# The up projection's entrance in another order: two snapshots at once, the norm's sums behind the fourth product, its spread behind the seventh

## Chip, core and metric

The kernel runs on one core of a Trainium2 chip. What counts is the device time of one execution in microseconds (us), the median over the runs shown; lower is better.

## What is computed

The reference is a whole block of a network on 1024 tokens of width 1024: a mixer with a residual, a gated feed-forward part with a short convolution, then a second block with latent attention and a Fourier mixer. The change lies where the feed-forward part begins:

```python
def rmsnorm(x, g, eps=EPS):
    xf = x.astype(jnp.float32)
    y = xf * lax.rsqrt(jnp.mean(xf * xf, axis=-1, keepdims=True) + eps)
    return (y * g.astype(jnp.float32)).astype(x.dtype)

def conv_ffn(h, w_up, conv_w, conv_b, w_down):
    gu = h @ w_up
    gate, up = gu[..., :D_FF], gu[..., D_FF:]
    gate = lax.conv_general_dilated(
        gate, conv_w[:, None, :], window_strides=(1,), padding=[(CONV_WIDTH - 1, 0)],
        dimension_numbers=('NWC', 'WIO', 'NWC'), feature_group_count=D_FF) + conv_b
    return (jax.nn.gelu(gate, approximate=False) * up) @ w_down

# in first_block
        x = x + merged @ w_out[l]
        x = x + conv_ffn(rmsnorm(x, ffn_norm_g[l]), w_up[l], conv_w[l], conv_b[l], w_down[l])
```

## The kernel before

Everything lies feature-major: 128 features on the partitions, 1024 tokens along the row. A float32 matrix product is made of three passes of matmuls over a high and a low part (`PASSES`), the high part being a rounded copy of the operand and the low part what is left of it. ScalarE (ACT) makes the high parts, VectorE (DVE) the low parts of the activations, GpSimd (POOL) the low parts of the weights (L689).

The up projection works in 22 pairs `p` of two 128-column blocks, one of the gate and one of the up half. Each pair is a 2 by 2 block product that is done with seven products of sums instead of eight. So a pair is seven products of 12 matmuls of 128x512 each (L1032), numbered n = 0 to 6 in the code; in words they are called product 1 to product 7 here. Product n multiplies `WS[n]` (weight sums, high and low part) with `OPERANDS[n]` (B11, BT1, B21, B22, BT2, BT4, BT3; BT are sums of quarters Y of the activations). Pairs take turns between two sets of three PSUM banks. Products 1, 5 and 7 add up in one bank, 2 and 4 in a second, 3 and 6 follow each other in the third. That is why copies and additions stand between them:

- ACT's `snap` copies a bank after product 1 (to FIRST), 2 (to KEEP), 5 and 6. Product 4 waits for the second snapshot, since it goes on adding in the bank of product 2 (`st_snap`, in `up_pair` of the tensor block).
- DVE's first addition of a pair (L2614, `GATE` from the bank of product 3 and FIRST) frees that bank. Product 6 opens it anew, so it waits for this addition: `pe.wait_ge(st_free, p * 3 + 7)`. The second addition (L2619) completes the other half of GATE, and L2622 multiplies it with the norm's factor, which PE has spread over all partitions in PSUM (`pair(3)`). From there go on the convolution (ACT L1812, DVE L2624 and L2626) and the gelu (L1817).

The norm's factor does not stand in the way of the products: they run on x times the gain, and the result is scaled afterwards. For it the squares are summed up in ACC; PE sums over the partitions with 8 narrow matmuls (`norm_sum`, L766), DVE turns the sum to a mean (L2592), ACT takes the root, DVE takes the reciprocal (L2597) and writes it on two diagonals (L2119), and PE spreads these (`norm_spread`, L774). GATE occupies the room in SBUF in which ACC lay, KEEP of the first pair that of Y22, and FIRST that of x.

Each engine runs its own list in the order in which the code writes it. The entrance is the stretch between the last matmuls of the output projection (L733) and the second pair's first product. On the tensor queue stand in a row: products 1 and 2, the norm sums, products 3 and 4, the spread, products 5 to 7, then the second pair. On DVE stand: the last sums of activations (L2508), low parts of BT2, mean, low parts of BT4, reciprocal, two diagonals, low parts of BT3, a memset, two sums of weights of the second pair (L2491, L2494), then the first addition. `late_hi` and `late_lo` are the high and low parts of BT2, BT4 and BT3, `high_part` those of `WS`, and `weight_sums` the sums from which WS are cast.

Of the kernel before, what the change touches and what calls it, by code (L numbers as in the profile page):

```python
# [10 lines left out]
ACT = mybir.ActivationFunctionType  # L11
# [3 lines left out]
T = 1024  # L15
D = 1024
KC = D // P
# [10 lines left out]
HK = KC // 2  # L28
FG = 8
HALF = T // 2  # L30
# [60 lines left out]
def before(phase, what):  # L91

    total = 0
    for name, adds in PHASES:
        if name == phase:
            return total
        total += adds.get(what, 0)
    raise KeyError(phase)
# [104 lines left out]
def build(nc, t_in, out):  # L203
# [105 lines left out]
    GATE = SC[:, 2:2 + T]  # L309
# [68 lines left out]
    lo = sem("lo")  # L378
# [74 lines left out]
    def operand_at(n, k):  # L453

        if n < 2:
            return 2 * k + n
        if n < 4:
            return 2 * HK + 2 * k + n - 2
        return 4 * HK + 2 * (n - 4) + k // 2
# [254 lines left out]
    def _(pe):  # L714
# [299 lines left out]
        def up_pair(p, q, first=False):  # L1014

            pe.wait_ge(st_free, p * 3 + 3)
            for n in range(PRODUCTS):
                if first and n == 2:
                    take(1, b("up", 1))
                pe.wait_ge(w_st, p * PRODUCTS + (n + 1))  # L1020
                if n == 3:
                    pe.wait_ge(st_snap, p * 4 + 2)
                elif n == 5:
                    pe.wait_ge(st_free, p * 3 + 7)
                elif n == 6:
                    pe.wait_ge(st_snap, p * 4 + 3)
                bank = BANKS[q][n]
                for k in range(HK):
                    if first:
                        pe.wait_ge(lo, before("out1", "split") + operand_at(n, k) + 1)  # L1030
                    for wp, xp in PASSES:
                        mm = pe.matmul(PS[:, bank:bank + HALF], WS[n][:, (wp * HK + k) * P:(wp * HK + k + 1) * P],  # L1032
                                       OPERANDS[n][:, (xp * HK + k) * HALF:(xp * HK + k + 1) * HALF],
                                       start=OPENS[n] and k == 0 and wp == 0 and xp == 0, stop=k == HK - 1 and wp == 1,
                                       skip_group_check=True)
                mm.then_inc(st_prod, 1)
                if first and n == 1:
                    norm_sum(before("norm2", "norm"), before("norm2", 2), early=before("norm2", "square") - 1)
                elif first and n == 3:
                    norm_spread(before("norm2", "norm"), before("norm2", 3))  # L1040

        take(0, b("up", 0))
# [425 lines left out]
    def _(act):  # L1468
# [232 lines left out]
        def attn_residual():  # L1701

            def operand_hi(dst, k, src):
                act.activation(dst[:, k * HALF:(k + 1) * HALF], src, ACT.Copy, scale=v1("ffn_g", k + (HK if dst is B21 or dst is B22 else 0))
                               ).then_inc(hi, 1)

            for c in range(KC):
                k, x, g = c % HK, TMP[c % 2], v1("ffn_g", c)
                pieces = ((B11, Y11), (None, Y12)) if c < HK else ((B21, Y21), (B22, Y22))
                for half in range(2):  # L1710
                    part = slice(half * HALF, (half + 1) * HALF)
                    dst, y = pieces[half]
                    if half == 0 or c == KC - 1:
                        act.wait_ge(x_new, before("out1", "xnew") + c + half + 1)
                    if dst is not None:
                        operand_hi(dst, k, x[:, part])
                    act.activation(y[:, k * HALF:(k + 1) * HALF], x[:, part], ACT.Copy, scale=g).then_inc(y_done, 1)
                    if c == KC - 1:
                        act.activation(SQ[:, part], x[:, part], ACT.Square).then_inc(sq_ready, 1)
                if c < KC - 1:  # L1720
                    act.activation(SQ, x, ACT.Square).then_inc(sq_ready, 1)
                if c == KC - 2:
                    high_part(0, 0, 0)
                    high_part(0, 1, 0)
                if c < HK:
                    act.wait_ge(t_sum, c + 1)
                    act.activation(BT1[:, k * HALF:(k + 1) * HALF], Y11[:, k * HALF:(k + 1) * HALF], ACT.Copy
                                   ).then_inc(hi, 1)
# [18 lines left out]
        def late_hi(n, sums):  # L1747

            dst, src = ((BT2, Y22), (BT4, Y21), (BT3, Y12))[n]
            for j in range(2):  # L1750
                part = slice(j * T, (j + 1) * T)
                act.wait_ge(t_sum, sums[j])
                act.activation(dst[:, part], src[:, part], ACT.Copy).then_inc(hi, 1)
# [22 lines left out]
        def snap(p, n, dst, bank):  # L1776
            act.wait_ge(st_prod, p * PRODUCTS + n)
            act.activation(dst, PS[:, bank:bank + HALF], ACT.Copy).then_inc(st_snap, 1)

        def ff_high(p, q, kept=None):  # L1780

            act.wait_ge(xt, p + xts[0] + 1)
            if kept is not None:
                act.wait_ge(st_prod, PRODUCTS * (FFC - 1) + 1)
            dst = FFS[q] if kept is None else FFD[kept]
            act.activation(dst[:, 0:T], PROD, ACT.Copy).then_inc(hi, 1)

        def up_pair(p, q, spilled=True, last=False, kept=None):

            def high_parts(first, end):  # L1790
                if not last:
                    for n in range(first, end):
                        high_part(p + 1, n, 1 - q)

            b_at, c_at, a_at = SUM_AT[q]
            snap(p, 1, FIRST[q], b_at)
            high_parts(0, 1)
            if isinstance(p, int) and p == 0:
                act.wait_ge(lo, before("out1", "split") + operand_at(4, HK - 1) + 1)
            if spilled:  # L1800
                act.wait_ge(ff_out, p * 16 - 16)
            snap(p, 2, KEEP[q][:, HALF:T], c_at)
            if isinstance(p, int) and p == 0:
                phase_norm("norm2")
                late_hi(2, (T3_SUMS[1], T3_SUMS[3]))
            else:
                ff_high(p - 1, 1 - q, kept)
            high_parts(1, 3)
            snap(p, 5, GATE[:, HALF:T], b_at)
            high_parts(3, 5)  # L1810
            act.wait_ge(gn_ready, p + 1)
            act.activation(CONV, SC[:, 0:T], ACT.Copy, scale=vec[:, bass.ds(p + VEC["conv0"], 1)]).then_inc(tap_ready, 1)  # L1812
            snap(p, 6, KEEP[q][:, 0:HALF], a_at)
            high_parts(5, 7)
            act.wait_ge(cv_ready, p + 1)
            act.wait_ge(lo, p + before("up", "split"))
            act.activation(PROD, CONV, ACT.Gelu, bias=vec[:, bass.ds(p + VEC["conv_b"], 1)]).then_inc(gl_ready, 1)  # L1817

        high_part(0, 2, 0)
        high_part(0, 3, 0)  # L1820
        late_hi(0, (T2_SUMS[1], T2_SUMS[3]))
        high_part(0, 4, 0)
        late_hi(1, (T4_SUMS[1], T4_SUMS[3]))
        high_part(0, 5, 0)
        high_part(0, 6, 0)
        act.wait_ge(done[2], before("norm2", 2) + 1)
        act.wait_ge(x_out, 16 * KC)
        up_pair(0, 0, spilled=False)
        act.wait_ge(lo, before("up", "split"))
        up_pair(1, 1, spilled=False)  # L1830
# [232 lines left out]
    def _(v):  # L2063
# [453 lines left out]
        def attn_residual():  # L2517
# [14 lines left out]
            def add_square(part):  # L2532
                sqs[0] += 1
                acs[0] += 1
                v.wait_ge(sq_ready, sqs[0])
                v.tensor_tensor(ACC[:, part], ACC[:, part], SQ[:, part], ALU.add).then_inc(sq_added, 1)
                v.wait_ge(sq_added, acs[0])
# [32 lines left out]
            v.wait_ge(y_done, 2 * c + 1)  # L2570
            operand_lo(B21, Y21, k * HALF, HALF)
            new_x(c, 1)
            add_square(halves[0])
            v.wait_ge(done[1], before("up", 1))
            weight_sums(0, 0, (2, 4))
            v.wait_ge(y_done, 2 * c + 2)
            operand_lo(B22, Y22, k * HALF, HALF)
            add_square(halves[1])
# [6 lines left out]
        def late_lo(dst, src):  # L2585
            for j in range(2):
                operand_lo(dst, src, j * T, T)

        v.wait_ge(t_sum, ts[0])
        late_lo(BT2, Y22)  # L2590
        v.wait_ge(done[2], before("norm2", 2) + 1)
        v.tensor_scalar(stat[:, 0:QT_N], PS[:, 2048:2048 + QT_N], 1.0 / D, 1e-6, ALU.mult, ALU.add).then_inc(ms_ready, 1)  # L2592
        v.wait_ge(ms_ready, before("norm2", "norm") + 1)
        v.sem_inc(free[2], 1)
        late_lo(BT4, Y21)
        v.wait_ge(sd_ready, before("norm2", "norm") + 1)
        chain(v.reciprocal(stat[:, 0:QT_N], stat[:, 0:QT_N]))  # L2597
        for a in (0, 4):
            diagonal(DIAG[:, a * P:(a + 4) * P], stat, a, a + 4).then_inc(diag_ready, 1)
        late_lo(BT3, Y12)  # L2600

        chain(v.memset(SC[:, 0:2], 0.0))

# [40 lines left out]
            v.tensor_tensor(dst[:, T:2 * T], PROD, dst[:, 0:T].bitcast(F32), ALU.subtract).then_inc(lo, 1)  # L2644
            v.wait_ge(lo, p + his[0] + 1)

        weight_sums(1, 1, (1, 3))
        up_pair(0, 0)
        up_pair(1, 1)
        with v.Fori(1, FFC // 2 - 1) as i:  # L2650
# [564 lines left out]
```

## Time and profile before

| | us |
|---|---|
| median of 3 runs | 2555.14 (2554.55 to 2556.97) |
| the profiled execution, its own time | 2560.54 |
| its span | 2558.7 |
| PE busy in it | 2468.8 (96%) |
| DVE busy | 1513.8 (59%) |
| ACT busy | 868.5 (34%) |
| POOL busy | 758.0 (30%) |

Times in the rows are us from the start of the span. The profiled execution took 5.4 us longer than the median; stretches are compared inside the trace and their difference is then laid on the median. In the timeline a row begins with its start and its length; matmuls overlap, so a row of twelve is 0.16 us longer than the step to the next product. The granted clock is a share of full speed, 1.00 for 2.4 GHz and 0.50 for 1.2 GHz.

### The profile page before, as it was taken

Reading aid. Unit: us, or ns where it says so; the run is one execution under the profiler, and the core shown is the slowest. Engines: PE = TensorE matmul, PEld = TensorE weight load, DVE = VectorE, ACT = ScalarE, POOL = GpSimd, SP = SyncE. Lnnn points to the kernel's source line nnn. Section 1 sums busy time; section 2 is a strip of 40 time slices with the busy share of each in tenths; the row PEclk is TensorE's granted clock in tenths of the full one; section 3 lists DMA queues with packets and bytes.
Section 4 is the critical chain, followed back from the end, with each engine's and each line's share of the span. In section 5 each row is a group of like instructions: output and inputs, shape, how many; then the busy total and the mean of one; then the engine's idle time right before and its main releaser. Section 6 shows DMA issues by size and latency. Waiting matters only on the chain.

```text
span 2558.7 us, 33196 instructions
## 1 busy us (share of the span) xinstructions
PE 2468.8 (96%) x12060; PEld 2035.9 (80%) x12060; DVE 1513.8 (59%) x1981; ACT 868.5 (34%) x1290; POOL 758.0 (30%) x442
## 2 busy tenths in 40 slices
PE   7999999999999999999999979999999989899997
PEld 5777787787787888888888868788888878688886
DVE  7856674735557877777411663377777764633454
ACT  4232222223224544445100232156666651222121
POOL 3232232332333555555344412200000003222221
PEclk9999999999999999999999989999999999999999
DMA  5134243421422223233553211100000002111112
GB/s 181 42 115 140 99 149 108 140 74 50 164 107 107 99 107 123 98 113 133 222 194 135 77 41 33 58 1 17 8 8 8 9 9 62 32 40 33 41 41 74
DMA packets 54417, 210.70 MB, mean 82 GB/s; under 512 B 6420, under 2 KB 7700, under 8 KB 49082
## 3 DMA queue, kind: packets, MB, share of 16 engines
q1 hardware_dynamic: 50340, 194.92, 22.0%
q10 hardware_dynamic: 3990, 14.59, 1.6%
q8 instruction: 57, 0.93, 0.1%
q14 instruction: 30, 0.25, 0.0%
HBM read 173.30 MB, written 38.55 MB: 83 GB/s over the span
## 4 chain that ended last, share of the span: by engine, by line
PE 84%; DVE 9%; issue 4%; ACT 1%; DMA 1%; POOL 1%; DVEq 0%; SPq 0%; ACTq 0%; POOLq 0%
PE PS L733 39%; PE PS L1032 16%; PE PS L1061 9%; PE PS L1277 4%; PE PS L1210 3%; PE PS L1216 2%; PE PS L1249 2%; PE PS L891 1%; PE PS L926 1%; DVE cols L2777 1%; PE PS L1200 1%; DVE SC L2327 1%; PE PS L766 1%; PE PS L774 1%; PE PS L1427 1%
## 5 line engine op out<-in xcount | busy, mean ns | idle before, releaser
L733 PE MATMUL PS<-H,w_hl 128*128 128x512 f32 x4512 | 1070.1, 396 | 31.8 <-DVE H L2142 9.4
L733 PEld LDWEIGHTS PS<-H,w_hl 128*128 128x128 f32 x4512 | 847.6, 190 | 231.7 <-issue 33.5
L682 POOL CAST w_hl<-w_raw 128x1024 fp32r<-128x1024 f32 x138 | 155.1, 1124 | 1546.7 <-PE PS L733 1011.8
L684 POOL TENSOR_TENSOR w_hl<-w_raw,w_hl 128x1024 fp32r<-128x1024 f32 x138 | 348.2, 2523 | 11.0
L1032 PE MATMUL PS<-BT,WS 128*128 128x512 f32 x1056 | 247.0, 389 | 0.0
L1061 PE MATMUL PS<-FFD,w_hl 128*128 128x512 f32 x1056 | 239.8, 389 | 0.1
L1032 PEld LDWEIGHTS PS<-BT,WS 128*128 128x128 f32 x1056 | 198.2, 188 | 41.6 <-issue 0.5
L1061 PEld LDWEIGHTS PS<-FFD,w_hl 128*128 128x128 f32 x1056 | 198.1, 188 | 41.6 <-DVEq L2450 0.5
L1032 PE MATMUL PS<-B,WS 128*128 128x512 f32 x792 | 190.7, 395 | 3.6 <-issue 3.6
L1032 PEld LDWEIGHTS PS<-B,WS 128*128 128x128 f32 x792 | 151.1, 191 | 35.7 <-issue 4.0
L689 POOL TENSOR_TENSOR WS<-w_raw,WS 128x512 fp32r<-128x512 f32 x88 | 140.3, 1605 | 73.1 <-ACT WS L1745 72.8
L1210 PE MATMUL PS<-CKV,QN 128*128 128x512 f32 (+1 forms) x576 | 142.1, 364 | 0.2 <-DVE PT L2793 0.2
L689 POOL TENSOR_TENSOR WS<-SUM,WS 128x512 fp32r<-128x512 f32 x66 | 98.3, 1503 | 122.3 <-ACT WS L1745 122.3
L2444 DVE TENSOR_TENSOR X<-PS,X 128x1024 f32 (+2 forms) x33 | 39.4, 1192 | 143.2 <-PE PS L1061 142.5
L1277 PE MATMUL PS<-PT,CKT 128*128 128x256 f32 x960 | 120.7, 283 | 1.5 <-DVE PT L2793 1.5
L1277 PEld LDWEIGHTS PS<-PT,CKT 128*128 128x128 f32 x960 | 117.8, 191 | 2.4 <-DVE PT L2793 1.7
L2793 DVE TENSOR_TENSOR PT<-PS,PT 128x512 fp32r<-128x512 f32 (+1 forms) x192 | 103.6, 596 | 23.5 <-ACT PT L1932 22.6
L1932 ACT ACTIVATE PT<-PS 128x512 fp32r<-128x512 f32 (+1 forms) x192 | 86.7, 523 | 76.1 <-PE PS L1249 76.1
L1210 PEld LDWEIGHTS PS<-CKV,QN 128*128 128x128 f32 x576 | 98.6, 188 | 17.3 <-DVE PT L2793 1.2
L2777 DVE TENSOR_REDUCE cols<-PS 128x1 f32<-128x1280 f32 x64 | 95.4, 1491 | 26.2 <-PE PS L1216 25.6
L1919 ACT ACTIVATE E<-PS,cols 128x1280 f32<-128x1280 f32 x64 | 85.3, 1333 | 51.6 <-DVE cols L2778 51.6
L1216 PE MATMUL PS<-KPE,QPS 128*128 128x512 f32 (+1 forms) x384 | 100.1, 355 | 0.0
(341 smaller groups left out, 3005.2 us busy)
## 6 DMA issues: line engine op xcount, KB each, us to landing
w_raw<-in_units SPq DMA_DIRECT2D x186, 512.0 KB, 3.6
AW<-in_ada SPq DMA_DIRECT2D x48, 512.0 KB, 4.2
ff_part<-FFS SPq DMA_DIRECT2D x20, 1024.0 KB, 4.9
FFD<-ff_part SPq DMA_DIRECT2D x20, 1024.0 KB, 5.6
X<-in_x SPq DMA_DIRECT2D x8, 512.0 KB, 8.7
x_part<-SC SPq DMA_DIRECT2D x8, 512.0 KB, 2.6
X<-x_part SPq DMA_DIRECT2D x4, 1024.0 KB, 8.7
out<-X SPq DMA_DIRECT2D x16, 256.0 KB, 2.1
```

The lines of the kernel that those rows point to most:

```text
L682: pool.tensor_copy(hi_part, raw).then_inc(w_hi, 1)
L684: pool.tensor_tensor(lo_part, raw, hi_part.bitcast(F32), ALU.subtract).then_inc(w_split, 1)
L689: pool.tensor_tensor(lo_part, ADDENDS[q][n][:, :], hi_part.bitcast(F32), ALU.subtract).then_inc(w_st, 1)
L733: mm = pe.matmul(PS[:, out_at + a:out_at + a + m], w(s, wp, w0 + k), src[:, o:o + m], start=(k == 0 and wp == 0 and xp == 0), stop=(k == k ...
L1032: mm = pe.matmul(PS[:, bank:bank + HALF], WS[n][:, (wp * HK + k) * P:(wp * HK + k + 1) * P], OPERANDS[n][:, (xp * HK + k) * HALF:(xp * HK ...
L1061: mm = pe.matmul(PS[:, out_at + a:out_at + a + 512], w(s, wp, w0 + k), FFD[home][:, xp * T + a:xp * T + a + 512], start=(k == 0 and wp == ...
L1210: mm = pe.matmul(PS[:, base + a:base + a + m], QN[:, qp_ * T + t * P:qp_ * T + (t + 1) * P], CKV[:, kp_ * TK + a:kp_ * TK + a + m], start= ...
L1216: mm = pe.matmul(PS[:, base + a:base + a + m], QPS[:, t * P:(t + 1) * P], KPE[:, kp_ * TK + a:kp_ * TK + a + m], start=False, stop=(kp_ == 1))
L1277: mm = pe.matmul(PS[:, 3584:3584 + GQ], CKT[:, vp * TK + kb * P:vp * TK + (kb + 1) * P], PT[:, xp * PTW + kb * GQ:xp * PTW + (kb + 1) * GQ ...
L1932: act.activation(block_cols(0, t, k0, k1), bank_cols(bank, k0, k1), ACT.Copy).then_inc(pt_hi, 1)
L2777: chain(v.tensor_reduce(cols[:, 22 + t % 2:23 + t % 2], PS[:, base:base + TK], AX, ALU.max))
L2793: v.tensor_tensor(block_cols(1, t, k0, k1), bank_cols(bank, k0, k1), block_cols(0, t, k0, k1).bitcast(F32), ALU.subtract).then_inc(pt_lo, 1)
```

## The change

It moves instructions on three engines and adds one copy on ACT; on PE and DVE nothing is added or removed. The norm sums go behind product 4 (n == 3, the fourth counted from one), the spread behind product 7 (n == 6). ACT casts WS[2] before the last half of x arrives, takes the snapshots of products 1 and 2 one behind the other as soon as the last x has been read, the second one into the spare FIRST[1], and copies it to KEEP later; the root comes behind the snapshot of product 5. DVE makes two sums of weights ahead of an addition of squares, all six low parts of BT2, BT4 and BT3 in a row ahead of the mean, and the second pair's sums of weights between mean and reciprocal. The first addition stays last.

```diff
@@ up_pair of the tensor block
-                if first and n == 1:
+                if first and n == 3:
                     norm_sum(before("norm2", "norm"), before("norm2", 2), early=before("norm2", "square") - 1)
-                elif first and n == 3:
+                elif first and n == 6:
                     norm_spread(before("norm2", "norm"), before("norm2", 3))
@@ scalar block, attn_residual
                         act.activation(SQ[:, part], x[:, part], ACT.Square).then_inc(sq_ready, 1)
+                        high_part(0, 2 + half, 0)
@@ scalar block, up_pair
-            snap(p, 1, FIRST[q], b_at)
-            high_parts(0, 1)
             if isinstance(p, int) and p == 0:
-                act.wait_ge(lo, before("out1", "split") + operand_at(4, HK - 1) + 1)
-            if spilled:
-                act.wait_ge(ff_out, p * 16 - 16)
-            snap(p, 2, KEEP[q][:, HALF:T], c_at)
-            if isinstance(p, int) and p == 0:
+                snap(p, 5, GATE[:, HALF:T], b_at)
                 phase_norm("norm2")
-                late_hi(2, (T3_SUMS[1], T3_SUMS[3]))
+                high_parts(0, 5)
             else:
...
@@ scalar block, ahead of the first pair
-        high_part(0, 2, 0)
-        high_part(0, 3, 0)
+        act.wait_ge(x_out, 16 * KC)
+        act.wait_ge(sq_ready, before("norm2", "square"))
+        snap(0, 1, FIRST[0], SUM_AT[0][0])
+        snap(0, 2, FIRST[1], SUM_AT[0][1])
         late_hi(0, (T2_SUMS[1], T2_SUMS[3]))
         high_part(0, 4, 0)
         late_hi(1, (T4_SUMS[1], T4_SUMS[3]))
         high_part(0, 5, 0)
         high_part(0, 6, 0)
+        late_hi(2, (T3_SUMS[1], T3_SUMS[3]))
+        act.wait_ge(lo, before("out1", "split") + operand_at(4, HK - 1) + 1)
+        chain(act.activation(KEEP[0][:, HALF:T], FIRST[1], ACT.Copy))
         act.wait_ge(done[2], before("norm2", 2) + 1)
-        act.wait_ge(x_out, 16 * KC)
         up_pair(0, 0, spilled=False)
@@ vector block
             new_x(c, 1)
-            add_square(halves[0])
             v.wait_ge(done[1], before("up", 1))
             weight_sums(0, 0, (2, 4))
+            add_square(halves[0])
...
         late_lo(BT2, Y22)
+        late_lo(BT4, Y21)
+        late_lo(BT3, Y12)
         v.wait_ge(done[2], before("norm2", 2) + 1)
...
-        late_lo(BT4, Y21)
+        weight_sums(1, 1, (1, 3))
         v.wait_ge(sd_ready, before("norm2", "norm") + 1)
...
-        late_lo(BT3, Y12)
...
-        weight_sums(1, 1, (1, 3))
         up_pair(0, 0)
```

The tensor queue at the entrance, one piece of the difference (B_103 to BT_109 are the seven operands, WS_114 to WS_120 the seven weights of the first pair):

```order
 L1032 MATMUL PS<-B_103,WS_114 128x512 x12
 L1032 MATMUL PS<-BT_104,WS_115 128x512 x12
-L766 MATMUL PS<-ones,SC 128x1 x8
 L1032 MATMUL PS<-B_105,WS_116 128x512 x12
 L1032 MATMUL PS<-B_106,WS_117 128x512 x12
-L774 MATMUL PS<-SC,ones 128x512 x2
+L766 MATMUL PS<-ones,SC 128x1 x8
 L1032 MATMUL PS<-BT_107,WS_118 128x512 x12
 L1032 MATMUL PS<-BT_108,WS_119 128x512 x12
 L1032 MATMUL PS<-BT_109,WS_120 128x512 x12
+L774 MATMUL PS<-SC,ones 128x512 x2
 L1032 MATMUL PS<-B_103,WS_114 128x512 x12
```

The sums now stand behind product 4, the spread behind product 7, right ahead of the second pair.

DVE before, from the low parts of BT2 to the first addition (Y_110, Y_112 and Y_113 are Y12, Y22 and Y21; stat holds the mean; w_raw_124 and SUM_121 belong to the second pair; SC holds GATE and FIRST):

```order
L2514 TENSOR_TENSOR BT_107<-Y_112,BT_107 128x1024 x2
L2592 TENSOR_SCALAR stat<-PS 128x8
L2514 TENSOR_TENSOR BT_108<-Y_113,BT_108 128x1024 x2
L2597 RECIPROCAL stat<-stat 128x8
L2119 TENSOR_TENSOR SC<-ident,stat 128x512 x2
L2514 TENSOR_TENSOR BT_109<-Y_110,BT_109 128x1024 x2
```

The same place in the changed kernel:

```order
L2518 TENSOR_TENSOR BT_107<-Y_112,BT_107 128x1024 x2
L2518 TENSOR_TENSOR BT_108<-Y_113,BT_108 128x1024 x2
L2518 TENSOR_TENSOR BT_109<-Y_110,BT_109 128x1024 x2
L2598 TENSOR_SCALAR stat<-PS 128x8
L2495 TENSOR_TENSOR SUM_121<-w_raw_124 128x512
L2498 TENSOR_TENSOR w_raw_124<-w_raw_124 128x512
```

The low parts moved ahead of the mean, and two sums of weights stand between the mean and the reciprocal; behind them follow reciprocal, diagonals, memset and the first addition.

## Rows read from the trace of the kernel before

**Rows 1.** The page, busy time of each engine over the span.

```profile
PE 2468.8 (96%) x12060; PEld 2035.9 (80%) x12060; DVE 1513.8 (59%) x1981; ACT 868.5 (34%) x1290; POOL 758.0 (30%) x442
```

**Rows 2.** The chain that ended last, 770 to 860 us: start, length, what.

```profile
825.54 34.50 PE PS L1032 x152
```

**Rows 3.** PE's timeline, 770 to 850 us: start, length, instructions, idle before.

```profile
802.22 2.88 PE L1032 MATMUL PS<-B,WS 128*128 128x512 f32 x12
...
807.66 0.94 PE L766 MATMUL PS<-ones,SC 128*128 128x1 f32 x8
809.31 1.35 PE L766 MATMUL PS<-ones,SC 128*128 128x1 f32 x8 [0.70 <-DVEq L2579]
810.52 4.32 PE L1032 MATMUL PS<-B,WS 128*128 128x512 f32 x12
818.47 5.35 PE L1032 MATMUL PS<-B,WS 128*128 128x512 f32 x12 [3.63 <-issue]
823.66 1.88 PE L774 MATMUL PS<-SC,ones 128*128 128x512 f32 x4
...
833.58 2.88 PE L1032 MATMUL PS<-B,WS 128*128 128x512 f32 x12
```

**Rows 4.** Windows of 1 us: length, PE busy, granted clock, DMA share, GB/s.

```profile
809.00:810.00 1.00, 0.69 (x6) 0.95 0.00 0
...
813.00:814.00 1.00, 1.00 (x5) 0.84 0.57 123
...
816.00:817.00 1.00, 0.00 (x0) 0.87 0.43 172
...
823.00:824.00 1.00, 1.00 (x4) 0.72 0.44 176
```

**Rows 5.** ACT's timeline: a square of x, snapshots of products 2, 5 and the next 2.

```profile
802.13 0.61 ACT L1719 ACTIVATE SC<-SC 128x512 f32<-128x512 f32 x1
...
817.79 0.58 ACT L1778 ACTIVATE KEEP<-PS 128x512 f32<-128x512 f32 x1
...
828.34 0.60 ACT L1778 ACTIVATE SC<-PS 128x512 f32<-128x512 f32 x1 [1.22 <-PE PS L1032]
...
839.22 0.60 ACT L1778 ACTIVATE KEEP<-PS 128x512 f32<-128x512 f32 x1
```

**Rows 6.** The last spill of x on the SP queue, and its time to landing.

```profile
804.64 0.33 SPq L558 DMA_DIRECT2D x_part<-SC  x1
...
x_part<-SC SPq DMA_DIRECT2D x1, 512.0 KB, 2.6
```

**Rows 7.** DVE's timeline, 803 to 845 us.

```profile
803.33 0.68 DVE L2514 TENSOR_TENSOR B<-Y,B 128x512 fp32r<-128x512 f32 x1
...
812.35 3.46 DVE L2514 TENSOR_TENSOR BT<-Y,BT 128x1024 fp32r<-128x1024 f32 x2
815.73 0.15 DVE L2592 TENSOR_SCALAR stat<-PS 128x8 f32<-128x8 f32 x1
...
820.40 2.15 DVE L2119 TENSOR_TENSOR SC<-ident,stat 128x512 f32<-128x512 f32 x2
822.48 2.35 DVE L2514 TENSOR_TENSOR BT<-Y,BT 128x1024 fp32r<-128x1024 f32 x2
824.77 0.06 DVE L2602 MEMSET SC<- 128x2 f32 x1
825.25 0.69 DVE L2491 TENSOR_TENSOR SUM<-w_raw 128x512 f32<-128x512 f32 x1 [0.41 <-DVE SC L2602]
...
826.58 0.69 DVE L2614 TENSOR_TENSOR SC<-PS,SC 128x512 f32<-128x512 f32 x1
...
831.02 1.22 DVE L2622 TENSOR_TENSOR SC<-SC,PS 128x1024 f32<-128x1024 f32 x1
...
844.26 0.69 DVE L2614 TENSOR_TENSOR SC<-PS,SC 128x512 f32<-128x512 f32 x1 [0.18 <-DVE FFS L2644]
```

**Rows 8.** POOL's timeline, 770 to 850 us: the low part of WS[4].

```profile
813.28 1.45 POOL L689 TENSOR_TENSOR WS<-SUM,WS 128x512 fp32r<-128x512 f32 x1 [2.96 <-ACT WS L1745]
```

More of the change, by code:

```diff
@@ L1795, in up_pair @@
             b_at, c_at, a_at = SUM_AT[q]
-            snap(p, 1, FIRST[q], b_at)
-            high_parts(0, 1)
             if isinstance(p, int) and p == 0:
-                act.wait_ge(lo, before("out1", "split") + operand_at(4, HK - 1) + 1)
-            if spilled:
-                act.wait_ge(ff_out, p * 16 - 16)
-            snap(p, 2, KEEP[q][:, HALF:T], c_at)
-            if isinstance(p, int) and p == 0:
+                snap(p, 5, GATE[:, HALF:T], b_at)
                 phase_norm("norm2")
-                late_hi(2, (T3_SUMS[1], T3_SUMS[3]))
+                high_parts(0, 5)
             else:
+                snap(p, 1, FIRST[q], b_at)
+                high_parts(0, 1)
+                if spilled:
+                    act.wait_ge(ff_out, p * 16 - 16)
+                snap(p, 2, KEEP[q][:, HALF:T], c_at)
                 ff_high(p - 1, 1 - q, kept)
-            high_parts(1, 3)
-            snap(p, 5, GATE[:, HALF:T], b_at)
-            high_parts(3, 5)
+                high_parts(1, 3)
+                snap(p, 5, GATE[:, HALF:T], b_at)
+                high_parts(3, 5)
             act.wait_ge(gn_ready, p + 1)
```

## Prediction

> **What bounds the kernel now.** The page comes first: PE is busy for 96% of the span [rows 1], so only time that PE loses or gains counts. The chain that ended last shows where: from 825.54 us on it is PE alone, product behind product [rows 2]. Whatever moves the second pair's first product, at 833.58 us, moves everything behind it. PE's timeline [rows 3] shows what the entrance costs. It begins at 802.22. Seven products at a step of 2.72 (a row of 2.88 less the overlap of 0.16) are 19.0 us, yet 31.4 pass. The rest is: the norm sums, 2.86 from 807.66 to 810.52, with a wait of 0.70 in them; 1.44 and 2.47 us that the rows of products 3 and 4 are longer than 2.88; 3.63 of idle time ahead of product 4; and the spread, from 823.66 until product 5. The clock rows [rows 4] tell why products 3 and 4 are long: the granted clock falls to 0.50 at 809.95, is back at 813.7, falls at 816.9 in the idle time and is back near 823.5. The idle time itself ends with the second snapshot, 817.79 + 0.58 = 818.37 [rows 5], so its releaser is ACT.
>
> Then the question that decides: what is late next? Product 6 began at 833.58 - 2 x 2.72 = 828.14 (ACT's snapshot of product 5, released by PE, begins at 828.34 [rows 5]), and DVE's first addition, which it waits for, had ended at 826.58 + 0.69 = 827.27 [rows 7]. That is 0.87 us of slack. So two chains reach product 6 almost together: PE's with its stalls, and DVE's list. The change shortens the first by much; I have to see what it does to the second.
>
> **Products 1 to 5.** WS[2] is cast ahead of the last half of x, in time in which ACT was idle. The snapshots wait for the last x to be spilled: issued at 804.64, 2.6 to land [rows 6], so 807.3. Product 2 ends at 807.8, both copies (0.58 each) by 809 to 809.5. Product 3 runs from 807.66 to 810.4, so product 4 starts without a wait and ends at 813.1; sums 2.15 (0.94 and 1.21 from [rows 3] without the wait), product 5 from 815.3 to 818.0, where it ended at 828.14 before. On PE alone that is 10.1 us won. If the clock falls behind the sums, 1.4 to 2.5 go, if x lands a little later, another bit: all of it costs nothing, since PE then waits.
>
> **Product 6 waits for DVE.** The changed list has the same members between the low parts of BT2 and the first addition, and the addition is still last. Its length from rows: six low parts of 1.18 (half of 2.35 [rows 7]), 7.05. GpSimd takes turns with them: the pair at 812.35 took 3.46 where the pair at 822.48, with GpSimd idle, took 2.35, so one low part of weights between two of DVE's costs 1.11. WS[4], WS[5] and WS[6] are cast by ACT in this time, so three turns, 3.3. Mean and its wait 0.3 (815.73 to 816.03). Two sums of weights 1.4. ACT's root needs the mean, and by then its table has long been loaded, so it hides behind these sums, and the reciprocal behind GpSimd. But behind the root ACT casts the second pair's WS[0] and WS[1], so two more turns of GpSimd lie around the diagonals, 2.2, and the diagonals are 1.3 (2.15 less the 0.85 of a turn in them). Memset with its wait 0.45, addition 0.7. Sum 16.7. Before it was 14.9 (812.35 to 827.27), with fewer turns of GpSimd in it.
>
> It starts when the last sum of activations is done. That was 812.3. Two sums of weights now run ahead of an addition of squares, which changes no total. ACT is free for the cast of WS[2] at about 802.65 (the square at 802.13, [rows 5]) and needs 0.6 for it, so GpSimd asks for its turn at about 803.3, and DVE's low part of B21 begins at 803.33 [rows 7]: a draw. If DVE goes first the list starts at 811.7, else at 812.6. Trace of before can't decide it; I take the middle, 812.15, and keep 0.45 to both sides. So the first addition ends at 828.85 and product 6 starts at 829.0, **0.86 later** than before: the 10.1 us have turned into idle time ahead of it.
>
> **The clock after that wait.** The idle time is 11 us; one of 3.6 sufficed for a fall [rows 4]. So product 6 begins at 1.2 GHz. The two rows at that level give 1.44 and 2.47, by how long it took to come back (2.9 and 5.1 us after the products resumed). I take 1.95, **+1.95**, bounds 1.4 and 2.9 (the last for products 6 and 7 together). Before, product 6 ran at full clock.
> The Trainium skill, TensorE: Matmul & The Clock Gate, Part 1, says the ramp is under 1% of a kernel's span and that a model need not fit it. By that the term would be dropped and the sum would be 2558.5. The rows agree on the share (0.08%), but of this change it is a third.
>
> **The spread.** It costs PE 1.76: from 823.66 to the 825.42 that lie three steps ahead of 833.58. Before it stood in the chain to product 6, now behind product 7: **+1.76** behind the wait. The second pair starts at 829.0 + 5.44 + 1.95 + 1.76 = 838.15, which is 4.57 after 833.58.
>
> **What is late next.** L2622 needs the spread. Before, the spread was done at 825.5 and L2622 ran at 831.02, when DVE came to it. Now it starts 0.17 into the second pair. From it to the end of the second pair's second snapshot it was 839.82 - 831.02 = 8.8 [rows 5, 7], over convolution and gelu; 0.15 of it waited for PE. So 8.65, and 0.1 to reach PE: 8.92 into the pair. Product 4 wants to begin at 8.16. **+0.76**. Product 6 of that pair wants the first addition: 844.95 - 831.02 = 13.93, so 14.2 into the pair, against 13.6 + 0.76: just in time. A pair later DVE has caught up.
>
> **Sum.** 0.86 + 1.95 + 1.76 + 0.76 = 5.33. On the profiled span of 2558.7 that is 2564.0; on the median, 2555.14 + 5.33 = **2560.5**. 0.2% is 5.1 us, about what a measurement of this kernel can tell from no change, so the forecast lies on this line. Lower bound: DVE wins the draw (-0.45), ACT's second cast comes too late for a turn between the diagonals (-1.1), clock 1.4 (-0.55), no stall in the second pair (-0.75): +2.5, 2557.6. Upper: +0.45, clock 2.9 (+0.95), one more turn of GpSimd in the second pair's DVE chain (+1.1): +7.8, 2563.
>
> **Rivals.**
> *Not slower: the front's gain survives.* Were the first addition done when product 5 ends, 818, the products would run through: product 7 ends at 823.5, the second pair starts at 825.2, 8.4 us sooner, 2546.8. What decides is when the addition ends: it breaks even at 828.85 - 5.33 = 823.5. For it speaks that nothing else holds PE's queue; against it that 16.7 less five turns, 11.2 us of DVE's own instructions, stand in front of the addition from 812.15 on, which is 823.3 at the very best. 4%.
> *GpSimd takes no turns.* Were the two engines not to exclude each other, the list would be 11.2 and the addition end at 823.3; the sum falls by 5.5 and the stall shrinks: about 2554.6. For it: the rows of instructions that read PSUM are not longer beside GpSimd. Against it: 3.46 beside 2.35, and 1.45 where GpSimd overlaps a low part [rows 7, 8]. 5%.
> The Trainium skill, SBUF — State Buffer, Who interferes with whom, calls this port pair an exclusive lock held for the whole instruction; the rows above agree, and by it all five turns stay.
> *DVE stays behind for longer.* With the second pair's chain late, a turn or two of GpSimd more, a stall at its product 6 too, and perhaps a fall of the clock there: 3 us on top, 2563.6. For it: DVE and GpSimd together fill most of a pair's 19 us. 13%.
> *The change doesn't do what it says*, x landing so late that product 4 still waits: worth nothing, the wait ahead of product 6 swallows up to 10 us. It is inside the forecast.
>
> **Chances.** Forecast 78%, the others as given. Inside the forecast a little over half lies above 2560.25: 41% slower, 37% same. With the third rival, slower 53%; with the second, same 42%; faster 5%. Range: the forecast's bounds, widened by the 1.2 us in which runs of before differ, and up to the third rival: 2556.4 to 2564.2.
>
> **What would show it.** Products 3 and 4 without idle time between, product 4 ending near 813; sums at 813; one idle stretch of 10 to 11 us ahead of product 6, released by DVE's first addition at 828 to 829.5; product 6 at clock 0.50 for 3 to 5 us; spread ahead of the second pair; its first product near 838; some 0.8 idle before its product 4. Wrong would be: no such idle stretch, the addition ahead of 824, or a stall in a third pair.

## The result and the profile after

The changed kernel takes 2562.31 us (median of 14, 2560.59 to 2564.24) where the kernel before, beside it, takes 2555.39 (14, 2552.89 to 2557.91): 6.9 us more, a ratio of 1.0025 with a 95% interval of 1.0017 to 1.0032. The profiled execution took 2563.18 us with a span of 2561.4.

One number is used from here on: the **entrance time**, from the start of the first pair's product 1 to the start of the third pair's product 1. Before it is 852.62 - 802.22 = 50.40 us, after it is 858.00 - 801.62 = **56.38**. So 5.98 of the 6.9 us lie in these fifty; the interval of the measurement, 4.3 to 8.2 us, holds both numbers. The two profiled spans differ by only 2.7 us, since the one of before was 5.4 above its median; the part of the traces outside the entrance is not compared here.

PE's timeline of the changed kernel, 770 to 870 us (start, length, instructions, idle before), answers to [rows 3]:

```profile
801.62 2.88 PE L1032 MATMUL PS<-B,WS 128*128 128x512 f32 x12
...
807.07 5.60 PE L1032 MATMUL PS<-B,WS 128*128 128x512 f32 x24
812.51 1.84 PE L766 MATMUL PS<-ones,SC 128*128 128x1 f32 x16
814.21 3.02 PE L1032 MATMUL PS<-BT,WS 128*128 128x512 f32 x12
828.71 7.76 PE L1032 MATMUL PS<-BT,WS 128*128 128x512 f32 x24 [11.48 <-DVEq L2620]
836.31 1.88 PE L774 MATMUL PS<-SC,ones 128*128 128x512 f32 x4
...
846.99 3.01 PE L1032 MATMUL PS<-B,WS 128*128 128x512 f32 x12 [0.60 <-ACT KEEP L1779]
...
858.00 2.88 PE L1032 MATMUL PS<-B,WS 128*128 128x512 f32 x12
```

Products 3 and 4 stand in one row of 24 without idle time, at full clock, and the sums behind them: the front of the entrance is as short as it was meant to be, and product 5 ends near 817.2. Then PE waits 11.48 us. The releaser is L2620, the semaphore that DVE raises behind its first addition. DVE's timeline of the changed kernel, over the same stretch, answers to [rows 7]:

```profile
802.73 0.68 DVE L2518 TENSOR_TENSOR B<-Y,B 128x512 fp32r<-128x512 f32 x1
...
811.20 10.21 DVE L2518 TENSOR_TENSOR BT<-Y,BT 128x1024 fp32r<-128x1024 f32 x6
821.33 0.15 DVE L2598 TENSOR_SCALAR stat<-PS 128x8 f32<-128x8 f32 x1
821.96 0.69 DVE L2495 TENSOR_TENSOR SUM<-w_raw 128x512 f32<-128x512 f32 x1 [0.48 <-DMA w_raw<-in_units]
822.69 1.64 DVE L2498 TENSOR_TENSOR w_raw<-w_raw 128x512 f32<-128x512 f32 x1
824.25 0.19 DVE L2603 RECIPROCAL stat<-stat 128x8 f32<-128x8 f32 x1
824.47 3.19 DVE L2123 TENSOR_TENSOR SC<-ident,stat 128x512 f32<-128x512 f32 x2
...
827.86 0.69 DVE L2619 TENSOR_TENSOR SC<-PS,SC 128x512 f32<-128x512 f32 x1 [0.19 <-DVE SC L2607]
...
838.22 1.22 DVE L2627 TENSOR_TENSOR SC<-SC,PS 128x1024 f32<-128x1024 f32 x1 [7.04 <-PE PS L774]
```

From 811.20 to 828.55 DVE works through its list without a longer break, and the addition is the last of it. The largest gap is 0.48 us behind the mean. Its row names a transfer of weights as releaser; the same 0.48 stands in the run with held casts with DVE's own mean as releaser, so the name is not certain. The clock, in windows of 1 us of the changed kernel (length, PE busy, granted clock, DMA share, GB/s), answers to [rows 4]:

```profile
819.00:820.00 1.00, 0.00 (x0) 0.72 0.91 168
...
832.00:833.00 1.00, 1.00 (x4) 0.50 0.00 0
833.00:834.00 1.00, 1.00 (x5) 0.96 0.00 0
```

It fell at 819.4, in the wait, and was back at 833.1, 4.4 us after product 6 began.

### The profile page after: what moved, and what is told of

Same layout as the page of the kernel before. It is cut to its first block, busy times and chain, and to the rows that moved or that the text cites. A ratio compares the mean times of both kernels' runs of the same rounds, so it can differ in the third digit from the quotient of the medians.

```text
span 2561.4 us, 33196 instructions
## 1 busy us (share of the span) xinstructions
PE 2465.3 (96%) x12060; PEld 2033.4 (79%) x12060; DVE 1514.0 (59%) x1981; ACT 868.7 (34%) x1291; POOL 756.3 (30%) x442
## 4 chain that ended last, share of the span: by engine, by line
PE 84%; DVE 11%; issue 3%; ACT 2%; DMA 1%; DVEq 0%; ACTq 0%; SPq 0%
PE PS L733 39%; PE PS L1032 16%; PE PS L1061 9%; PE PS L1277 4%; PE PS L1210 3%; PE PS L1216 2%; PE PS L1249 2%; PE PS L891 1%; PE PS L926 1%; DVE cols L2781 1%; PE PS L1200 1%; DVE SC L2331 1%; PE PS L766 1%; PE PS L774 1%; PE PS L1427 1%
## 5 line engine op out<-in xcount | busy, mean ns | idle before, releaser
L1210 PEld LDWEIGHTS PS<-CKV,QN 128*128 128x128 f32 x576 | 98.6, 188 | 16.7 <-DVE PT L2797 0.6
```

What stands on the lines that cost most here:

```text
L1210: mm = pe.matmul(PS[:, base + a:base + a + m], QN[:, qp_ * T + t * P:qp_ * T + (t + 1) * P], CKV[:, kp_ * TK + a:kp_ * TK + a + m], start= ...
```

## The experiments

Each edit is against the changed kernel unless it says otherwise. "Addition" is the end of DVE's first addition, counted from the start of product 1; it is 25.05 before the change (827.27 - 802.22) and 26.93 after it (828.55 - 801.62). Ratios are against the kernel before, run beside it.

### The spread behind product 6

```diff
-                elif first and n == 6:
+                elif first and n == 5:
                     norm_spread(before("norm2", "norm"), before("norm2", 3))
```

> The changed kernel with the spread behind product 6 instead of product 7. Entrance time here and below: from the start of product 1 of the first pair to the start of product 1 of the third pair; 50.40 us before the change (802.22 to 852.62), 56.38 after it (801.62 to 858.00). My theory (product 6 waits for DVE's first addition; the spread then stands in front of what DVE does for the second pair): product 6 starts as before at 27.1, the spread costs its 1.76 as before, but L2622 can run 2.7 us earlier, so the 0.60 to 0.8 of idle time ahead of the second pair's product 4 go: 55.5. Rival (that stall is DVE's backlog from elsewhere): 56.4, no change. Rival (the spread is hidden there): 53.7.

PE's timeline of this run:

```profile
799.37 2.88 PE L1032 MATMUL PS<-B,WS 128*128 128x512 f32 x12
...
826.47 4.85 PE L1032 MATMUL PS<-BT,WS 128*128 128x512 f32 x12 [11.49 <-DVEq L2620]
831.16 1.88 PE L774 MATMUL PS<-SC,ones 128*128 128x512 f32 x4
...
841.08 5.60 PE L1032 MATMUL PS<-B,WS 128*128 128x512 f32 x24
...
854.68 2.88 PE L1032 MATMUL PS<-B,WS 128*128 128x512 f32 x12
```

Entrance 854.68 - 799.37 = 55.31, 1.07 less. Products 3 and 4 of the second pair now run through (one row of 24): the stall there came from the spread standing late, not from a backlog of DVE. The spread's own cost stays. Product 6 starts at 27.10 (826.47 - 799.37), as in the changed kernel (27.09). The ratio is 1.0020 (1.0010 to 1.0029), too wide to tell 1 us.

### Matmuls for nothing in the wait

```diff
+                elif first and n == 4:
+                    pe.wait_ge(w_st, 6)
+                    for j in range(44):
+                        pe.matmul(PS[:, 1536:2048], WS[5][:, 0:P], B22[:, 0:HALF], start=True, stop=True,
+                                  skip_group_check=True)
```

> The changed kernel with 44 more matmuls of 128x512 behind product 5, into a PSUM bank that nobody reads (their result is thrown away), some 10 us of the 11.48 us that PE waits. It takes the low clock away from product 6 and adds nothing to any other engine. My theory: the addition still ends at 26.9, product 6 starts at 27.1, products 6 and 7 take 5.44 instead of 7.60: entrance 54.2. Rival (the clock is not what makes them long, or the fall comes anyway in the last 1.5 us of waiting): 56.4.

PE's timeline of this run:

```profile
801.12 2.88 PE L1032 MATMUL PS<-B,WS 128*128 128x512 f32 x12
...
816.57 10.13 PE L1042 MATMUL PS<-B,WS 128*128 128x512 f32 x44
828.34 5.70 PE L1032 MATMUL PS<-BT,WS 128*128 128x512 f32 x24 [1.64 <-issue]
...
855.57 2.88 PE L1032 MATMUL PS<-B,WS 128*128 128x512 f32 x12
```

Product 6 starts at 27.2, where it did, but products 6 and 7 take 5.70 instead of 7.76. Entrance 54.45: the low clock is worth 1.9 to 2.1 us, and the wait itself is not touched by it. Ratio 1.0018 (1.0008 to 1.0027).

### The second pair's casts held back

```diff
                 phase_norm("norm2")
+                act.wait_ge(st_free, 7)
                 high_parts(0, 5)
```

> The changed kernel with ACT's casts of the second pair's weights held back until DVE's first addition is done, so that GpSimd takes no turns between DVE's sums of weights, diagonals and addition. My theory: three turns of 0.95 to 1.1 us go, the addition ends 2.5 to 3.2 us earlier after the start of product 1 (24.1 instead of 26.9), product 6 follows it at once: entrance 53.5. Rival (GpSimd and DVE don't exclude each other, the long rows have another cause): 56.4. Rival (held casts are late for the second pair): above 54.5 with idle time in front of the second pair.

DVE's timeline of this run, rows behind the mean:

```profile
820.11 0.69 DVE L2496 TENSOR_TENSOR SUM<-w_raw 128x512 f32<-128x512 f32 x1 [0.48 <-DVE stat L2599]
820.84 0.69 DVE L2499 TENSOR_TENSOR w_raw<-w_raw 128x512 f32<-128x512 f32 x1
...
821.67 1.29 DVE L2124 TENSOR_TENSOR SC<-ident,stat 128x512 f32<-128x512 f32 x2
...
823.17 0.69 DVE L2620 TENSOR_TENSOR SC<-PS,SC 128x512 f32<-128x512 f32 x1 [0.19 <-DVE SC L2608]
```

The second sum of weights takes 0.69 instead of 1.64, the two diagonals 1.29 instead of 3.19: together 2.85 less, which is three turns of GpSimd at 0.95. The addition is at 823.86 - 799.82 = 24.04, the entrance 53.19. The rival without exclusion falls, and so does the one of late casts: no idle time stands in front of the second pair, and the entrance is under 54.5. Ratio 1.0008 (0.9999 to 1.0018).

### DVE's order undone, the rest kept

```diff
         late_lo(BT2, Y22)
-        late_lo(BT4, Y21)
-        late_lo(BT3, Y12)
         (mean)
-        weight_sums(1, 1, (1, 3))
+        late_lo(BT4, Y21)
         (reciprocal, diagonals)
+        late_lo(BT3, Y12)
         chain(v.memset(SC[:, 0:2], 0.0))
+        weight_sums(1, 1, (1, 3))
```

> The changed kernel with DVE's order behind the low parts of BT2 as it was before the change: mean, BT4, reciprocal, diagonals, BT3, memset, two sums of weights, first addition. Tensor queue and ACT stay changed. My theory: what counts is that the first addition is last behind the same list, not the order in the list; it ends within 1 us of 26.9, entrance 55.4 to 57.4. Rival (the low parts moved ahead of the mean are to blame, since the root waits for them): the addition is back at 25.0 and the entrance at 54 or below.

A miss: the addition is at 824.88 - 799.62 = 25.26 and the entrance 54.47, outside what my theory gave, and just short of what the rival gave (25.0, and 54 or below). The order in the list does count for 1.7 us. But it leaves 4.1 of the 6.0 us, and PE still waits 9.82 ahead of product 6. Ratio 1.0022 (1.0012 to 1.0031). Which part of the order it is was asked next.

### Only the two sums of weights put back

```diff
-        weight_sums(1, 1, (1, 3))
         v.wait_ge(sd_ready, before("norm2", "norm") + 1)
...
         chain(v.memset(SC[:, 0:2], 0.0))
+        weight_sums(1, 1, (1, 3))
```

> The changed kernel with one thing of DVE's order put back: the two sums of the second pair's weights stand behind the memset again, not between mean and reciprocal; all low parts stay ahead of the mean. Question left by the run with DVE's whole order undone, whose addition ended 1.7 us earlier. Theory: the sums ahead of the diagonals release ACT's casts, and so GpSimd's turns, before the diagonals; behind the memset they are cast after the addition, and only one turn (WS[0]) lies in the list. The addition ends at 25.2 to 25.5, entrance 54.3 to 54.8. Rival (the low parts ahead of the mean cost it): the addition stays near 26.9, entrance 56.4.

GpSimd's timeline of this run, and behind it the same stretch of the changed kernel:

```profile
821.63 1.49 POOL L689 TENSOR_TENSOR WS<-w_raw,WS 128x512 fp32r<-128x512 f32 x1 [4.27 <-ACT WS L1746]
825.52 1.27 POOL L689 TENSOR_TENSOR WS<-SUM,WS 128x512 fp32r<-128x512 f32 x1 [2.40 <-ACT WS L1746]
```

```profile
822.32 1.45 POOL L689 TENSOR_TENSOR WS<-w_raw,WS 128x512 fp32r<-128x512 f32 x1 [4.27 <-ACT WS L1746]
823.74 1.71 POOL L689 TENSOR_TENSOR WS<-SUM,WS 128x512 fp32r<-128x512 f32 x1
825.41 1.70 POOL L689 TENSOR_TENSOR WS<-w_raw,WS 128x512 fp32r<-128x512 f32 x1
```

Here the addition ends at 826.10 - 800.94 = 25.16, entrance 54.29. It is as early as with DVE's whole order undone (25.26), so all of the 1.8 us come from where the two sums stand, and the low parts ahead of the mean cost nothing here. Early, the two sums release the cast of WS[1], and those of WS[1] and WS[2] put two more GpSimd turns around the diagonals. Behind the memset only WS[0] falls into the list. Ratio 1.0021 (1.0012 to 1.0030).

### Three terms at once

The held casts, 32 matmuls for nothing behind product 5, and the spread behind product 6.

> The changed kernel with three terms taken away at once: 32 thrown-away matmuls behind product 5 that keep the clock up, the second pair's casts held until the first addition is done, the spread behind product 6. If the terms add up (theory): the addition ends at 24.1, product 6 starts at 24.2, no low clock, no stall: entrance 50.4, as before the change, and the time within 0.1% of it. Rival (they hide one another): 52 or more.

The addition is at 24.12 (824.30 - 800.18), product 6 at 24.3, entrance 50.63; ratio 0.9999 (0.9990 to 1.0008). Taken away alone, the three gave 3.19, 1.93 and 1.07 us, a sum of 6.19; taken away at once they give 56.38 - 50.63 = 5.75. So they add up but for 0.4 us, and all but 0.2 of the loss of 5.98 is back. That is not the loss taken apart by its causes: the spread still costs its 1.76 us, and the held casts give more (the addition 2.8 earlier) than the 1.17 by which product 6 was late.

### The early snapshots alone, in the kernel before

```diff
         high_part(0, 3, 0)
+        act.wait_ge(x_out, 16 * KC)
+        act.wait_ge(sq_ready, before("norm2", "square"))
+        snap(0, 1, FIRST[0], SUM_AT[0][0])
+        snap(0, 2, FIRST[1], SUM_AT[0][1])
...
-            snap(p, 2, KEEP[q][:, HALF:T], c_at)     (first pair)
+                chain(act.activation(KEEP[0][:, HALF:T], FIRST[1], ACT.Copy))
```

> The kernel before with the early snapshots alone (both taken as soon as the last x is spilled, the second by way of FIRST[1]); tensor queue, DVE's order and the casts as before. Theory (product 6 hangs on DVE's first addition, which had 0.87 us of slack): product 4 starts 3 to 4 us earlier, but the spread then waits for the diagonals and product 6 for the addition, at a clock that has fallen: entrance 50.4 to 53. Rival (the snapshots' wait was what bound the entrance): 46 to 47.

PE's timeline of this run:

```profile
800.09 2.88 PE L1032 MATMUL PS<-B,WS 128*128 128x512 f32 x12
...
808.08 7.32 PE L1032 MATMUL PS<-B,WS 128*128 128x512 f32 x24
819.96 3.75 PE L774 MATMUL PS<-SC,ones 128*128 128x512 f32 x4 [4.57 <-DVE SC L2126]
822.73 9.98 PE L1032 MATMUL PS<-BT,WS 128*128 128x512 f32 x36
...
851.59 2.88 PE L1032 MATMUL PS<-B,WS 128*128 128x512 f32 x12
```

DVE's and ACT's timelines of this run, the first addition and the snapshot of product 5:

```profile
824.45 0.68 DVE L2621 TENSOR_TENSOR SC<-PS,SC 128x512 f32<-128x512 f32 x1
```

```profile
827.31 0.60 ACT L1778 ACTIVATE SC<-PS 128x512 f32<-128x512 f32 x1 [2.32 <-PE PS L1032]
```

Product 4 follows product 3 at once, the 3.63 us of idle time are gone, and 4.57 appear ahead of the spread, which waits for DVE's diagonals. It then runs at the low clock and takes 3.75 instead of 1.88. Entrance 51.50, 1.1 more than before; ratio 1.0004 (0.9995 to 1.0013): nothing won. DVE's list is where it was: the addition ends at 825.13 - 800.09 = 25.04. The entrance lies in the forecast range, but one part of the theory missed: product 6 did not wait for the addition. PE came to it at 827.1 (832.55 - 2 x 2.72), 2.0 us after the addition had ended, held up by the wait for the diagonals and by the clock, which was low until 825.3. At full clock PE would have been there at 819.96 + 1.76 + 2.72 = 824.4 by the steps of the kernel before, and the addition would have been the next wait; that is worked out and not shown by this run.

### The first addition early

```diff
         late_lo(BT2, Y22)
-        late_lo(BT4, Y21)
-        late_lo(BT3, Y12)
         (mean)
+        v.wait_ge(st_prod, 3)
+        v.wait_ge(st_snap, 1)
+        chain(v.tensor_tensor(GATE[:, 0:HALF], PS[:, SUM_AT[0][2]:SUM_AT[0][2] + HALF], FIRST[0], ALU.add))
+        v.sem_inc(st_free, 1)
+        late_lo(BT4, Y21)
+        late_lo(BT3, Y12)
         weight_sums(1, 1, (1, 3))
```

> The changed kernel with the mean and the first addition right behind the low parts of BT2; GATE may be written there, since the norm's sums have been read by then. If the wait for this addition is the cause, product 6 starts as soon as the low parts of BT4 are there, about 19 after product 1 instead of 27.1; product 7 ends near 24, the spread waits a little for the diagonals: the second pair starts at 27.4 instead of 36.4, entrance 47.3, 2552 us. Rival (something else on PE's queue is late as well): above 52.

PE's timeline of this run:

```profile
799.48 2.88 PE L1032 MATMUL PS<-B,WS 128*128 128x512 f32 x12
...
817.15 3.01 PE L1032 MATMUL PS<-BT,WS 128*128 128x512 f32 x12 [0.52 <-DVE BT L2518]
...
823.77 1.10 PE L774 MATMUL PS<-SC,ones 128*128 128x512 f32 x2 [1.60 <-DVE SC L2123]
825.36 2.08 PE L774 MATMUL PS<-SC,ones 128*128 128x512 f32 x2 [0.49 <-DVE SC L2123]
...
847.80 2.88 PE L1032 MATMUL PS<-B,WS 128*128 128x512 f32 x12
```

The 11.48 us are gone; PE now waits half a microsecond at a time for low parts and 2.1 for the diagonals. In that wait the clock falls, and the second pair's product 1 takes 4.36 instead of the 3.33 that it takes behind the spread in the changed kernel. Entrance 48.32, 1.0 more than expected and 2.1 less than before. The time, 2556.22 us, 0.9997 (0.9988 to 1.0006), can't tell a gain of 2.1 us (0.9992) from none.

### The diagonals and the spread earlier too

As the run before it, but DVE does the diagonals ahead of the low parts of BT3, the sums of weights come last, and the spread stands behind product 6.

> As the run with the early addition, but the diagonals ahead of the low parts of BT3 and the spread behind product 6. Theory: product 7 waits for BT3 until about 23, the second pair starts near 25.5, no stall in it: entrance 44.5 to 46, 2550 us, faster than both kernels. Rival: BT3's low parts so late that nothing is won over the early addition alone, 47.3.

PE's timeline of this run, the second pair:

```profile
824.80 2.88 PE L1032 MATMUL PS<-B,WS 128*128 128x512 f32 x12
...
836.91 5.37 PE L1032 MATMUL PS<-B,WS 128*128 128x512 f32 x12 [3.80 <-ACT KEEP L1779]
```

A miss. The second pair does start at 24.7 (824.80 - 800.13), but its product 4 waits 3.80 us for a snapshot and then runs at the low clock. Entrance 50.20, ratio 0.9995 (0.9986 to 1.0004): neither what my theory gave nor faster. The snapshot stands on ACT behind the first pair's convolution and gelu.

### What stopped the second pair moved as well

```diff
             snap(p, 6, KEEP[q][:, 0:HALF], a_at)
-            high_parts(5, 7)
+            if isinstance(p, int) and p == 0:
+                high_parts(3, 7)
+                snap(1, 1, FIRST[1], SUM_AT[1][0])
+                snap(1, 2, KEEP[1][:, HALF:T], SUM_AT[1][1])
+            else:
+                high_parts(5, 7)
...
             v.tensor_tensor(GATE, GATE, pair(3), ALU.mult).then_inc(gn_ready, 1)
+            if first:
+                weight_sums(1, 1, (2, 4))
...
             v.tensor_tensor(PROD, PROD, GATE, ALU.mult).then_inc(xt, 1)
+            if first:
+                v.wait_ge(xt, xts[0] + 1)
+                v.wait_ge(st_prod, PRODUCTS + 3)
+                v.wait_ge(st_snap, 5)
+                chain(v.tensor_tensor(GATE[:, 0:HALF], PS[:, SUM_AT[1][2]:SUM_AT[1][2] + HALF], FIRST[1], ALU.add))
+                v.sem_inc(st_free, 1)
```

This edit is against the run before it. The lines that take the two snapshots, the sums and the addition out of their old places are left out.

> The kernel with the early addition, diagonals ahead of BT3 and spread behind product 6, and with what then stopped the second pair (3.80 us idle ahead of its product 4, for a snapshot queued behind convolution and gelu) moved too: ACT takes the second pair's first two snapshots ahead of the gelu, DVE does second addition and L2627's multiplication ahead of the next sums of weights, and the second pair's first addition right behind the first pair's last multiplication. Theory: the second pair starts at 24.7, no idle time ahead of its products 4 and 6: entrance 43.7 to 45, 5.4 to 6.7 us below the kernel before, 2550 us. Rival (a wait only moves on again): a stall of 2 us or more ahead of the second pair's product 6, entrance above 46.

PE's timeline of this run:

```profile
800.27 2.88 PE L1032 MATMUL PS<-B,WS 128*128 128x512 f32 x12
...
824.97 2.88 PE L1032 MATMUL PS<-B,WS 128*128 128x512 f32 x12
...
830.41 5.60 PE L1032 MATMUL PS<-B,WS 128*128 128x512 f32 x24
...
844.01 2.88 PE L1032 MATMUL PS<-B,WS 128*128 128x512 f32 x12
...
853.60 3.03 PE L1032 MATMUL PS<-B,WS 128*128 128x512 f32 x12 [1.26 <-ACT KEEP L1779]
```

The second pair runs through. Entrance 43.74, 6.7 us below the kernel before; 1.26 of it are given back ahead of product 4 of the third pair, so a part of the wait did move on, behind the end of the entrance. The time is 2551.80 us against 2555.81 beside it, ratio 0.9981 (0.9972 to 0.9990): 4.0 us below, a little more than half of what was gained in the entrance; 5.4 of it are left behind that stall, and the interval, 2.6 to 7.2, holds that too. It is faster than the kernel before, and so than the changed one, whose ratio to it is 1.0025.

## Why the prediction was right

I forecast 2560.5 us, 5.3 above the kernel before, and 2556.4 to 2564.2; it is 2562.31, 6.9 above. Step by step, from the trace:

| Step | predicted | measured |
|---|---|---|
| product 6 starts later by | 0.86 | 1.17 (27.09 against 25.92) |
| low clock on products 6 and 7 | 1.95 | 2.16 (7.60 against 5.44) |
| spread behind product 7 | 1.76 | 1.76 (836.31 to 838.07) |
| stall ahead of the second pair's product 4 | 0.76 | 0.76 (846.99 against 838.07 + 8.16) |
| sum | 5.33 | 5.98, with 0.13 behind that product |

838.07 is where the spread's row leaves off in PE's steps: product 2 of the second pair starts at 840.79, less one step of 2.72.

- **What is late next.** The step on which all hung held: 0.87 us of slack at product 6 is all that could be won at the front, and the rest became 11.48 us of idle time. The early addition removes the wait. The snapshots alone, in the kernel before, won nothing either, though there the diagonals and the clock held PE before the addition could.
- **The length of DVE's list** was the term that was sized too small. It was 17.35 us (811.20 to 828.55) against 16.7. Row by row: low parts 10.13 against 10.35 counted; mean with its wait 0.63 against 0.3; sums of weights, reciprocal and diagonals 5.65 against 4.9; memset with its wait 0.25 against 0.45. I had counted two turns of GpSimd behind the mean; there were three. I counted ACT's casts of WS[0] and WS[1] and not that of WS[2], which needs no sum and follows at once. Held casts give the price, 2.85 for three. ACT's timeline of the changed kernel shows the cast of WS[2], right behind that of WS[1] at 822.69 and with no wait:

```profile
823.22 0.61 ACT L1746 ACTIVATE WS<-w_raw 128x512 fp32r<-128x512 f32 x1
```

- **The draw** for the low part of B21 went to DVE (0.68 long, the next instruction 0.60 behind), so the list began 0.35 us earlier than the middle that I took: 9.58 us after product 1 (811.20 - 801.62) against 9.93. The list was 0.65 longer, so product 6 came 0.3 later than forecast. That the two errors partly cancel is luck.
- **The order in the list** I held for indifferent, in the expectation of the run with DVE's order undone. It is not: where an instruction stands decides when another engine is released, and that engine then takes turns with it.
- **The clock** came back 4.4 us after product 6 began, between the two rows on which the term rested. Behind the norm sums it did not fall at all. My reading of its first return in the kernel before was off: by the row of 0.84 it was back at 813.3, not at 813.7, and by the row of 0.87 it fell at 816.7, not at 816.9. No term rests on these.
- **The rivals.** *The front's gain survives* is excluded by the wait. *GpSimd takes no turns* fell with the held casts. *DVE stays behind for longer* did not come: the second pair's product 6 lost nothing to a wait, and in the third pair all products follow each other. The stated chances are a point off: 41 and 13 make 54% for slower, which leaves 4% for faster.
- The 0.9 us between the entrance and the measured difference were not traced; they are inside the interval.

## What to carry to other kernels

Before a stall is taken away, find the wait that ends just before the next instruction and read its slack; the gain is that slack, not the stall. A list that decides a wait is as long as its own instructions plus the turns of the engine that shares its port, so count what every moved instruction releases elsewhere. And an instruction on which PE waits belongs as early in its queue as its data allow, not where its stage stands in the text: that move alone showed no gain in the time (0.9997), but with those that it made necessary, in the spread, the diagonals and the second pair, it turned a loss of 7 us into a gain of 4.

## What the runs showed of the hardware

DVE and GpSimd took turns when both had work: six low parts of DVE took 10.21 us with three of GpSimd's instructions among them, 7.05 of it their own by the row of 2.35 for two [rows 7], so 1.05 a turn. By the steps in the trace the second, third and fourth of the six took about 2.2 us each and the others 1.1, so no two of GpSimd's went in between the same two of DVE's. That is the exclusive lock that the Trainium skill describes (SBUF — State Buffer, Who interferes with whom), here with its price. In the run with the snapshots alone the spread took 3.75 us at the low clock against 1.88. ACT loaded the root's table at 818.05, ahead of its wait for the mean, and ran the root at 821.52, as ACT's timeline of the changed kernel shows:

```profile
818.05 1.28 ACT L1473 ACT_TABLE_LOAD   x1
821.52 0.21 ACT L1473 ACTIVATE stat<-stat 128x8 f32<-128x8 f32 x1 [2.19 <-DVE stat L2598]
```

So the load of 1.28 us cost nothing, since it stood in idle time ahead of the wait.
